# Modulation and input projection as one phase in a hybrid diffusion step

## What is computed

```python
mod_ctx = (silu(c_ctx) @ w_ada + b_ada)            # (6*1024,); the same with c for the latent tokens
shift1, scale1, gate1, shift2, scale2, gate2 = split(mod, 6)
h = norm(x) * (1 + scale1) + shift1                # norm: over the 1024 channels
z = h @ w_in                                       # w_in (1024, 2304)
za, zb, q, k, v = split(z)                         # 512, 256, 3 x 512 columns
z = gelu(za); u, v_ = split(z)                     # mixer A, chunks of 128 tokens
v_ = norm(v_); v_ = einsum(ws, v_) + bs; out_a = u * v_
# mixer B: 2-D DFT of zb; mixer C: neighbourhood attention over q, k, v with a position bias rpb
# then output projection, layer norm, gated convolutional feed-forward, layer norm
```

## Time and profile before

| | before |
|---|---|
| median of 3 runs | 3072.39 us (3071.53 to 3072.41) |
| the profiled execution | 3068.97 us, span 3067.2 us |
| mean granted clock of TensorE | 0.959 of full speed |
| TensorE busy (matmul) | 2806.9 us, 92% of the span |
| VectorE busy | 1833.8 us, 60% |
| ScalarE busy | 1278.1 us, 42% |
| moved by the transfer engines | 432.54 MB, mean 141 GB/s |

### The profile page before, as it was taken

How to read it: one execution, slowest core, us unless ns; L and a number is a source line. 1 busy time by engine, 2 the same in 40 slices (tenths; PEclk the granted TensorE clock), 3 DMA queues, 4 the chain that set the end, 5 groups by cost and what they waited for, 6 DMA issues and landing times. The chain is left out here.

```text
span 3067.2 us, 51638 instructions
## 1 busy us (share of the span) xinstructions
PE 2806.9 (92%) x17742; PEld 2545.9 (83%) x17742; DVE 1833.8 (60%) x3176; ACT 1278.1 (42%) x2746; POOL 411.8 (13%) x589
## 2 busy tenths in 40 slices
PE   1899999857999997999699999999999979999997
PEld 1799999746888886787599999999999968888875
DVE  4443432155989897576778786666766633453545
ACT  3111111114888786122455565555655532121121
POOL 0000000032222221123200000000000000311312
PEclk6899999978999998999799999999999989999998
DMA  7322222398446531545465556444444445243233
GB/s 254 97 88 84 96 78 76 103 376 199 89 97 137 123 89 46 176 157 190 105 216 168 166 170 204 150 148 158 152 149 150 146 139 165 84 139 125 94 127 130
DMA packets 372881, 432.54 MB, mean 141 GB/s; under 512 B 91918, under 2 KB 267870, under 8 KB 370016
## 3 DMA queue, kind: packets, MB, share of 16 engines
q1 hardware_dynamic: 352383, 415.00, 43.6%
q10 hardware_dynamic: 18720, 9.44, 1.0%
q0 software_dynamic: 1600, 5.77, 0.5%
HBM read 307.92 MB, written 124.19 MB: 141 GB/s over the span
## 5 line engine op out<-in xcount | busy, mean ns | idle before, releaser
L2065 PE MATMUL fu_alpha<-fu_h,fu_w 128*128 128x384 f32 x3168 | 575.0, 336 | 19.2 <-DVE fu_h L2291 10.6
L2065 PEld LDWEIGHTS fu_alpha<-fu_h,fu_w 128*128 128x128 f32 x3168 | 554.0, 189 | 21.3 <-issue 21.3
L2551 PE MATMUL fd_acc<-fd_w,fd_f 128*128 128x512 f32 x2376 | 546.5, 392 | 27.2 <-DVE fd_w L2579 17.9
L2551 PEld LDWEIGHTS fd_acc<-fd_w,fd_f 128*128 128x128 f32 x2376 | 447.4, 189 | 126.2 <-issue 18.0
L2065 PE MATMUL fu_beta<-fu_h,fu_w 128*128 128x384 f32 x1584 | 285.4, 334 | 0.7 <-DVE fu_h L2291 0.7
L2065 PEld LDWEIGHTS fu_beta<-fu_h,fu_w 128*128 128x128 f32 x1584 | 275.5, 188 | 1.1 <-issue 1.1
L552 PE MATMUL pj_gps<-pj_ht,w_in 128*128 128x256 f32 x2160 | 268.1, 284 | 0.0
L552 PEld LDWEIGHTS pj_gps<-pj_ht,w_in 128*128 128x128 f32 x2160 | 262.7, 192 | 1.3
L2575 DVE TENSOR_TENSOR fd_f<-fd_f_stage,fd_f 128x512 fp32r<-128x512 f32 (+1 forms) x110 | 91.5, 833 | 283.8 <-ACT fd_f L2531 283.8
L2531 ACT CAST fd_f<-fd_f_stage 128x512 fp32r<-128x512 f32 (+1 forms) x110 | 63.6, 579 | 443.4 <-PE fd_acc L2551 391.0
L2265 DVE TENSOR_TENSOR fu_w<-up_w_stage,fu_w 128x512 fp32r<-128x512 f32 x264 | 181.5, 689 | 84.8 <-ACT fu_w L2129 81.9
(11 more groups left out here) (207 smaller groups left out, 4224.4 us busy)
## 6 DMA issues: line engine op xcount, KB each, us to landing
up_w_stage<-in_w_gu_dram SPq DMA_DIRECT2D x88, 512.0 KB, 4.2
fu_w_sums<-w_gu_sums SPq DMA_DIRECT2D x132, 256.0 KB, 3.3
fd_w_stage<-in_w_down_dram SPq DMA_DIRECT2D x54, 512.0 KB, 3.7
fd_f_stage<-f_t SPq DMA_DIRECT2D x88, 256.0 KB, 2.6
at_k<-k_t SPq DMA_DIRECT2D x28, 704.0 KB, 12.8
w_gu_sums<-fu_w_sums SPq DMA_DIRECT2D x66, 256.0 KB, 4.7
fo_w<-in_w_ada_dram SPq DMA_DIRECT2D x8, 2048.0 KB, 14.9
up_w_stage<-in_w_gu_dram SPq DMA_DIRECT2D x44, 256.0 KB, 4.5
```

The lines of the kernel that those rows point to most:

```text
L2065: mm = pe.matmul(out, w[x][:, j, k, :], b[y][:, j, k, :], start=opens and (k, x, y) == (0, HI, HI), stop=(k, x, y) == (KH - 1, LO, HI), sk ...
L2551: mm = pe.matmul(acc[:, t, at], f[a][:, slot, t * P:(t + 1) * P], w[b][:, w_at(st, slot), at], start=is_step(st, 0) and (a, b) == (HI, HI) ...
```

## The change

The modulation moves into `projection_phase`; `mod` no longer holds shift1 and scale1, and there is no phase boundary in between.

- Transfers on SP, in order: the conditioning vectors, `w_ada` chunk 0, x of group 0, chunk 1, then `w_in` block 0, chunk 2, block 1, chunk 3, block 2, x of group 1 (once group 0's transposes are done), blocks 3 to 8, `rpb_pad`, `rel_bias`, x of group 2.
- `w_in` comes in nine blocks of 128 x 8 x 256 (1 MB, rows of 1,024 bytes) straight into `w_raw`, which lies over the low half `w[LO]`; `high_w(n)` on ScalarE and `low_w(n)` on VectorE (in place) split a block at a time. In group 0 a product waits only for as many blocks as it needs (`USE_BLOCKS`).
- The constants, `b_ada` and the setup's small weights are loaded through ScalarE's queue.
- The modulation product goes to `gps` slot 2 with 32 columns of silu (30 of them zero), is copied to SBUF by ScalarE, turned by four transposes on TensorE, and four small VectorE operations add the bias and 1 straight into `shift` and `scale1p`.
- All 16 transposes of group 0 go out at once: the last two pairs use the free `abps` buffer. The first product waits for the pairs of `ht` one by one instead of for all four.
- `norm_x(1)` stands ahead of the modulation on VectorE.

```diff
+    W_BLOCK = 256
+    W_BLOCKS = [col // W_BLOCK for col in (COL_ZA, COL_ZA + 256, COL_Q, COL_ZB, COL_Q + 256, COL_K, COL_K + 256, COL_V, COL_V + 256)]
+    USE_BLOCKS = (2, 3, 4, 4, 5, 6, 7, 9, 9)
...
+        with nc.sbuf_tensor("ada_w", [P, 2, KT, ADA_COLS], F32) as wa:
+            pass
         ht = [sb(f"pj_ht{h}", [P, 2, KT, G_TOK], F32R) for h in (HI, LO)]
...
+        late_pairs = abps[:, :, :].rearrange("p a (k t) -> p a k t", k=2)
+
+        def turned(n, j):
+
+            return late_pairs[:, j - 2] if isinstance(n, int) and n == 0 and j >= 2 else tps[:, j % 2]
...
                 sp.sem_inc(lo_stored, 16)
                 sp.sem_inc(v_stored, 16)
-                with nc.allow_non_contiguous_dma(reason="modulation and biases, channel on partition"):
-                    for v in range(2):
-                        for dst, what in ((shift, SHIFT1), (scale, SCALE1)):
-                            sp.dma_start(dst[:, v, :], mod[v, what * D:(what + 1) * D].rearrange("(k p) -> p k", p=P)).then_inc(consts_loaded, 16)
-                    sp.dma_start(bs[:, :], a_bs.rearrange("l h p -> p (l h)")).then_inc(consts_loaded, 16)
-                sp.dma_start(ident[:, :], ident_in).then_inc(consts_loaded, 16)
-
-                sp.dma_start(zbt[:, 0, 0:P], dft_c64).then_inc(consts_loaded, 16)
-                sp.dma_start(zbt[:, 1, 0:P], dft_s64).then_inc(consts_loaded, 16)
...
+                with nc.allow_non_contiguous_dma(reason="conditioning vectors, channel on partition"):
+                    for v in (LAT, CTX):
+                        sp.dma_start(cond[:, v, :], conds[v].rearrange("(k p) -> p k", p=P)).then_inc(cond_loaded, 16)
+                sp.dma_start(wa[:, 0], ada_cols[0]).then_inc(wa_loaded[0], 16)
+                sp.dma_start(x[:, :, :], x_groups[0]).then_inc(x_loaded, 16)
+                sp.dma_start(wa[:, 1], ada_cols[1]).then_inc(wa_loaded[1], 16)
+
+                def load_w(n):
+                    sp.dma_start(w_raw[:, :, w_at(n)], w_rows[:, :, w_at(n)]).then_inc(w_loaded[n], 16)
+
+                for n in range(2, N_ADA):
+                    load_w(n - 2)
+                    sp.wait_ge(ada_done, n - 1)
+                    sp.dma_start(wa[:, n % 2], ada_cols[n]).then_inc(wa_loaded[n % 2], 16)
+                load_w(2)
                 sp.wait_ge(tps_done, SUB)
                 sp.dma_start(x[:, :, :], x_groups[1]).then_inc(x_loaded, 16)
+                for n in range(3, len(W_BLOCKS)):
+                    load_w(n)
+                sp.dma_start(rpb_pad[:, RPB_PAD:RPB_PAD + RPB], rpb.rearrange("l h r c -> l (h r c)")).then_inc(rpb_stored, 16)
+                sp.wait_ge(zeroed, 1)
+                for at in (0, RPB_PAD + RPB):
+                    sp.dma_start(rpb_pad[:, at:at + RPB_PAD], zeros[:, :]).then_inc(rpb_stored, 16)
+                sp.wait_ge(rpb_stored, 48)
                 shifted = bass.AP(rpb_pad.tensor, RPB_PAD + REL_COLS // 2, [[REL_COLS, HEADS * REL_ROWS], [-1, GRID], [1, GRID]])
                 sp.dma_start(rel_bias.rearrange("q r k -> r q k"), shifted).then_inc(rel_stored, 16)
...
+                act.dma_start(ident[:, :], ident_in).then_inc(consts_loaded, 16)
+                act.dma_start(zbt[:, 0, 0:P], dft_c64).then_inc(consts_loaded, 16)
...
+                act.dma_start(ws[:, :, :].rearrange("p a (b q) -> p (a b) q", q=P), a_ws.rearrange("l h p q -> p (l h) q")).then_inc(fw_loaded, 16)
+                act.wait_ge(fw_zeroed, 1)
+                for g in range(4):
+                    pair, half = g // 2, g % 2
+                    act.dma_start(fw2[half * 64:half * 64 + 64, pair * P + half * 64:pair * P + half * 64 + 64],
+                                  f_w[0, g]).then_inc(fw_loaded, 16)
+                act.wait_ge(cond_loaded, 32)
+                act.wait_ge(silu_zeroed, 1)
+                act.activation(silu[:, :, 0:2].rearrange("p k v -> p v k"), cond[:, :, :], ACT.Silu).then_inc(silu_done, 1)
+
+                with nc.allow_non_contiguous_dma(reason="biases, channel on partition"):
+                    act.dma_start(mod_bias[:, :], b_ada[0, 0:2 * D].rearrange("(k p) -> p k", p=P)).then_inc(mod_bias_loaded, 16)
+                    act.dma_start(bs[:, :], a_bs.rearrange("l h p -> p (l h)")).then_inc(consts_loaded, 16)
...
+                def high_w(n):
+                    act.wait_ge(w_loaded[n], 16)
+                    act.copy(w[HI][:, :, w_at(n)], w_raw[:, :, w_at(n)]).then_inc(w_hi, 1)
+
+                high_w(0)
+                high_w(1)
+                act.wait_ge(ada_done, N_ADA)
+                act.copy(ada_row, ada_acc).then_inc(ada_copied, 1)
+                high_w(2)
                 for j in range(SUB):
                     round_h(0, 0, j)
+                for n in range(3, len(W_BLOCKS)):
+                    high_w(n)
...
+                def ada_product(n):
+
+                    pe.wait_ge(wa_loaded[n % 2], (n // 2 + 1) * 16)
+                    for k in range(KT):
+                        for q in range(ADA_STRIPS):
+                            mm = pe.matmul(ada_acc[q * STRIP_ROWS:(q + 1) * STRIP_ROWS, n * ADA_STRIP:(n + 1) * ADA_STRIP], silu[:, k, :],
+                                           wa[:, n % 2, k, q * ADA_STRIP:(q + 1) * ADA_STRIP],
+                                           start=k == 0, stop=k == KT - 1, tile_position=(0, q * STRIP_ROWS))
+                    mm.then_inc(ada_done, 1)
+
+                pe.wait_ge(silu_done, 1)
+                for n in range(2):
+                    ada_product(n)
...
-                    if not (isinstance(n, int) and n == 0 and j < 2):
+                    if not (isinstance(n, int) and n == 0):
...
+                for n in range(2, N_ADA):
+                    ada_product(n)
+                pe.wait_ge(ada_copied, 1)
+                for n in range(N_ADA):
+                    mm = pe.transpose(gps[:, 1, n * P:(n + 1) * P], ada_row[:, n * P:(n + 1) * P], ident[:, :])
+                mm.then_inc(ada_turned, 1)
...
+                        if first_group:
+                            pe.wait_ge(w_lo, USE_BLOCKS[unit[0]])
...
+                            if first_group and unit[0] == 1 and k % 2 == 0:
+                                pe.wait_ge(h_lo, k // 2 + 1)
...
                     if isinstance(g, int) and g == 0:
-                        pe.wait_ge(h_lo, SUB)
                         rows(0, COL_ZA)
...
                 norm_x(0)
                 dve.wait_ge(consts_loaded, 16 * N_CONSTS)
-                dve.tensor_scalar(scale1p[:, :, :], scale[:, :, :], 1.0, None, ALU.add).then_inc(scale_done, 1)
...
-                dve.wait_ge(scale_done, 1)
+
+                def low_w(n):
+                    dve.wait_ge(w_hi, n + 1)
+                    at = w_at(n)
+                    dve.tensor_tensor(w[LO][:, :, at], w_raw[:, :, at], w[HI][:, :, at].bitcast(F32), ALU.subtract).then_inc(w_lo, 1)
+
+                low_w(0)
+                low_w(1)
+                norm_x(1)
+                dve.wait_ge(mod_bias_loaded, 16)
+                dve.wait_ge(ada_turned, 1)
+                for v in range(2):
+                    of = lambda ap: ap.rearrange("p (n q) -> p n q", n=2)
+                    dve.tensor_tensor(of(shift[:, v, :]), ada_t[:, 0:2, :, v], of(mod_bias[:, 0:KT]), ALU.add).then_inc(scale_done, 1)
+                    dve.scalar_tensor_tensor(of(scale1p[:, v, :]), ada_t[:, 2:4, :, v], 1.0, of(mod_bias[:, KT:2 * KT]), ALU.add, ALU.add).then_inc(scale_done, 1)
+                dve.wait_ge(scale_done, 4)
                 modulate(0, 0, LAT)
-                norm_x(1)
+                for n in range(2, 4):
+                    low_w(n)
 
...
                     gate_norm(0)
                     low_qk(0, 1, HD ** -0.5)
+                    if isinstance(g, int) and g == 0:
+                        for n in range(4, len(W_BLOCKS)):
+                            low_w(n)
                     if next2:
...
-            w = [ctx.enter_context(nc.sbuf_tensor(f"w_in{h}", [P, KT, P_IN], F32R)) for h in (HI, LO)]
-            modulation_phase(nc, conds, w_ada, b_ada, w_in, rpb, mod, rpb_pad, w)
-            projection_phase(nc, x_all, w, a_ws, a_bs, f_w, ident, dft_c64, dft_s64,
-                             mod, rpb_pad, rel_bias, y, q_t, k_t, v_parts, chan_dft, new_k, new_v)
+            w_high = ctx.enter_context(nc.sbuf_tensor("w_in0", [P, KT, P_IN], F32R))
+            with nc.sbuf_tensor("w_in_raw", [P, KT, P_IN], F32) as w_raw:
+                pass
+            w = [w_high, ctx.enter_context(nc.sbuf_tensor("w_in1", [P, KT, P_IN], F32R))]
+            projection_phase(nc, conds, w_ada, b_ada, w_in, rpb, x_all, w, w_raw, a_ws, a_bs, f_w, ident, dft_c64, dft_s64,
+                             rpb_pad, rel_bias, y, q_t, k_t, v_parts, chan_dft, new_k, new_v)
```

125 lines of the change are left out of this document (25 added, 100 removed).

## The result

The changed kernel takes **3047.15 us** (median of 4 runs, 3045.71 to 3049.27) against 3071.96 us for the kernel before, timed beside it (4 runs, 3066.99 to 3072.41). The ratio is 0.992, with a 95% interval from 0.9908 to 0.9932: 24.8 us faster by the medians. The two profiled executions, 3068.97 and 3046.25 us, differ by 22.7 us; the prediction had 22.0 for this difference, and 3050.4 us for the median.

The account below looks back on a forecast made before the run. TensorE was taken to pace the groups, so the end follows their start. Mix product at 101.3 instead of 125.73 us, 24.4 earlier, less 2.4 for the clock: 22.0 off the 3072.4 median gives 3050.4 us, 8-in-10 range 3043 to 3061.

Parts of the forecast that it names:

- What bounds the kernel: Whole kernel: TensorE paces the groups, so the end follows their start; mix product 24.4 us earlier, net gain 22.0 us.
- When x of group 1 lands: Load stream: 14.16 MB at 390 GB/s, 2.0 us for the bias and 0.9 delay, from 4.0, give 43.2 us.
- When the modulation is ready: Start: ready at 43.2 us; fourth chunk lands at 37.8, its product takes 3.6, copy and four transposes about 1.8.
- Asking late for x costs nothing, being last in the queue does: SP's queue: group 1's x, asked for at 31.7 us, waits behind a w_ada chunk and a w_in block anyway.
- No saving in transfer by ScalarE's queue: Constant loads: ScalarE issuing them saves no transfer time; were they free, the sum would be 1.3 us less.
- The normalisation lies bare on the path: VectorE ahead of group 0's modulation: group 1's normalisation adds 5.5 us to the path, ending at 48.7.
- The rival that it is covered: VectorE at the start: group 1's normalisation is hidden, 5.5 us off the path, 3045 us; chance 0.13.
- ScalarE's six casts, 58.8 to 69.8: Ahead of group 1's modulation: ScalarE rounds w_in blocks 3 to 8 in a row, 1.83 us each, VectorE waiting.
- The rival that blocks cost more than the earlier trace: w_in casts: 2.6 us a block on ScalarE and VectorE, 6.3 us more, 3057, or 3060 with slower transfers; chance 0.17.
- GELU to mix: VectorE in group 0: 79.9 to 101.3 us, including 11.1 of low halves; TensorE waits some 9 us.
- The clock behind the wait, 2.4: TensorE behind the mix product: five microseconds at half clock cost about 2.4 us of the 24.4 gained.
- The slower rival by the transfer of 1,024-byte rows: w_in loads: the change loses if a block takes over 6.1 us; at 134 GB/s 7.8 us, 3088; chance 0.03.

Follow-up runs that it names:

- e3_no_bias_load: Changed kernel with the shift and scale bias taken as zero and its load of 2,048 four-byte elements dropped; 3047.39 us.
- e4_consts_sp: Changed kernel with the ten small constant and bias loads on SP's queue, behind the first w_in block, instead of ScalarE's; 3052.63 us.
- e8_consts_pool: Changed kernel with the constants and both biases issued by GpSimd instead of ScalarE; 3050.05 us.
- e10_turn_late: Changed kernel with group 0's 16 transposes behind the modulation products of chunks 2 and 3 instead of ahead of them; 3053.68 us.
- e1_norm_late: Changed kernel with group 1's normalisation put back behind group 0's modulation on VectorE; 3042.4 us.
- e2_gate_first: Changed kernel with tile 1's gate behind one low half, ahead of the other four and group 2's statistics, GpSimd's small powers reordered to match; 3034.78 us.
- the second profile: The changed kernel run and profiled once more, nothing altered; median 3049.85 us, profiled execution 3051.62 us.
- the whole reordering: Changed kernel with the same work reordered on VectorE, ScalarE, TensorE and GpSimd up to the mix product, including the earlier gate of tile 1; 3027.29 us.
- e6_rows512: Changed kernel with each w_in block loaded in two halves, in rows of 512 bytes instead of 1,024; 3051.52 us.

## Why the prediction was right, and where its steps were off

- **What bounds the kernel** (the start of the groups; the milestone at the mix; nothing given back later): right for the start. The shift at v, 22.0, stands through the last phase to within 0.8 us in the first profile of the change; in the second 3.7 of its 21.0 us are lost behind the projection, as the same program varies there.
- **When x of group 1 lands**: predicted 43.2, measured 45.19, the largest miss on the path. Its error is in two terms that lean opposite ways. The bias load costs 1.2 on the stream (`e3_no_bias_load`), where I took 2.0; the share of 0.58 over five microseconds is 2.9 us of a full stream, and half of it, 1.5, would have been nearer. The 14.16 MB, which I took at 390 GB/s from the earlier trace rows, needed 45.19 - 4.0 - 0.9 - 1.2 = 39.1 us, 362 GB/s. The row length is part of it: at 348 instead of 390 a block takes 3.0 us instead of 2.7, 0.9 for three. The other 1.9 no run takes apart; part of it may be the constants, since in `e4_consts_sp`, where they come behind it, the second `w_ada` chunk's product starts at 18.49 instead of 20.75. By the Trainium skill ("DMA: Bandwidth & Descriptors", section "Why small descriptors are slow") 1,024-byte rows should be some 4% slower than 2,048-byte ones and 512-byte rows some 8% slower than 1,024-byte ones, estimates from its 3 cycles a packet. The traces have 348 against 403 GB/s, 14%, and 290 against 348, 17%, and the measurement decides.
- **When the modulation is ready**: predicted 43.2 as well, measured 42.96, by two errors that cancel. The fourth chunk's product starts at 39.65, where I had its chunk land at 37.8, and takes 1.96 us instead of 3.6. So the order of the two arrivals, x behind the modulation by 2.2 us, is measured, but the prediction had them at the same moment.
- **Asking late for x costs nothing, being last in the queue does**: right as far as it went. In `e8_consts_pool` x was asked for 4.9 us earlier (31.71) and landed no earlier (statistics at 45.49). But the step named no point at which it stops being true. `e10_turn_late` puts a request at 45.99, and there it costs 5.8.
- **No saving in transfer by ScalarE's queue**: the bytes indeed come no faster, and I priced the queue at nothing. That was wrong in what it left out: SP is freed of issues that are held up, worth 2.4 us at the mix (`e4_consts_sp`). By the Trainium skill ("DMA: Bandwidth & Descriptors", section "Issuing engines are not separate DMA queues") several issuers save only issue time, "usually small relative to the DMA itself". The first half agrees with `e8_consts_pool`, where a third engine issues the loads and x lands within 0.3 us of the change; the second does not hold for SP beside this stream, where a 64 KB load took 5.46 us to issue.
- **The normalisation lies bare on the path**: right. It took 5.4 us of VectorE, from 45.19 to the adds at 50.58; undone, 4.3 come back at v (`e1_norm_late`), though that edit also takes the wait for x off the modulation. The rival that it is covered was wrong.
- **Four adds at 1.0**: 0.4 measured (50.58 to 50.99). With x 2.0 late, modulation starts 1.3 late (50.99 for 49.7).
- **ScalarE's six casts, 58.8 to 69.8**: measured 59.98 to 70.88, 1.82 each, and the last block is in time. The rival that blocks cost more than the earlier trace rows was wrong: a 128x2048 block in eight pieces costs the same as one in a row (1.82 and 2.22 us for 1.83 and 2.22 in the earlier trace rows). VectorE's wait ended at 71.43; ScalarE's cast of the waiting pair, which releases it, starts at 70.79 (predicted 69.8).
- **GELU to mix**: five low halves 11.09 for 11.1, wait 9.52 for "some 9", mix 102.02 for 101.3. `e2_gate_first` shows that this backlog is the cause, since with the gate ahead of it the wait is gone.
- **The clock behind the wait, 2.4**: 1.7 in one profile of the change and 2.7 in the other (13.94 from mix to v before, 15.65 and 16.63 after); 2.4 lies inside the 1.5 to 2.7 of the eight profiles with that wait.
- **The slower rival by the transfer of 1,024-byte rows** is out by far: a block takes 3.0 us, not 6.1, and even 512-byte rows (290 GB/s) move the mix by only 2.2 and v by 2.8.

The mechanism was right; that the sum was as close as 22.0 for 22.7 is in part luck. The late x (+2.0) was offset by the smaller adds (-0.6), by several small steps up to the mix that together took 0.7 less, and by a smaller loss to the clock (-0.7); with the clock of the second profile the shift at v is 21.0, and with its later phases 17.3 at the end. The median of the change lies 3.3 us under the number given, about what the medians of one kernel differ by (3047.15 and 3049.85).

## What to carry to other kernels

When a load phase is folded into a compute phase, the gain at the first product is not the gain at the end: follow each in-order engine past it and look for deferred work (here six casts, then five subtractions) that stands ahead of a small operation on which the bounding engine waits. Moving such a gate ahead of the backlog took a few lines and gave 11 us; the whole reordering gave 20. And a prefetch must be judged in both directions: work put early "while a transfer arrives" is only hidden if its own input is not the last thing that the transfer brings.

## What the runs showed of the hardware

- The rate of a full stream falls with the row length: 403 GB/s with rows of 2,048 and 4,096 bytes, 348 with 1,024, 290 with 512 (5 to 12 of `e4_consts_sp`, 44 to 60 of the change, 48 to 64 of `e6_rows512`). The busy share rises in the same order: 1.04, 1.10, 1.18.
- A small load of four-byte elements on ScalarE's queue beside a full stream landed late: the 8 KB bias 18.1 us after its issue, the 2 KB `pj_bs` behind it 21.8, where the first constant took 2.5. Without the bias ahead of it `pj_bs` took 11.8 (`e3_no_bias_load`); on GpSimd's queue the two took 7.9 and 7.2 (`e8_consts_pool`), so it is not so for every second queue. TensorE's setup products waited 4.58 us for `pj_bs`, without consequence here.
- Issuing is held up when much is under way: 5.46 us for a 64 KB load on SP (`e4_consts_sp`), 6.75 for a 1 MB block on SP and 10.30 for the 2 KB load on ScalarE in the change, 0.4 to 0.9 for issues that are not held up.
- Two executions of one program that both reached the mix at 102.02 after the same wait were granted different clocks behind it: the same 48 products took 6.77 and 7.77 us. The medians of the two sets of runs of this kernel lie 2.7 us apart; that the clock is the cause of that is not shown.
